# Seven block products in another order on three bank pairs, with the weight differences and loads spread over the chunks before them

## What is computed

```
def conv_glu_ffn(h_norm, w_in, conv_w, conv_b, w_out):
    gate, up = jnp.split(h_norm @ w_in, 2, axis=-1)
    ...
    return (jax.nn.silu(conv) * up) @ w_out      # 512 x 2816 times 2816 x 1024

h = h + conv_glu_ffn(rms_norm(h, norm_ffn[l]), ...)
```

## Time and profile before

| | us |
|---|---|
| median of three runs | 1417.26 |
| lowest, highest | 1415.71, 1418.31 |
| the profiled execution | 1415.03 |
| its span | 1413.3 |
| PE busy in it | 1388.4 (98%) |
| DVE, ACT, POOL busy | 879.0, 648.7, 666.3 |

### The profile page before, as it was taken

The page is one execution under the profiler, slowest core; times in us unless marked ns, Lnnn a source line. Parts: engine busy times, 40 slices in busy tenths (PEclk is TensorE's granted clock), DMA queues, the critical chain, the costliest instruction groups (busy, mean ns, idle before and its releaser), DMA issues.

```text
span 1413.3 us, 17598 instructions
## 1 busy us (share of the span) xinstructions
PE 1388.4 (98%) x6797; PEld 1135.6 (80%) x6797; DVE 879.0 (62%) x1249; ACT 648.7 (46%) x1109; POOL 666.3 (47%) x365
## 2 busy tenths in 40 slices
PE   8999999999999999999999999999999999999998
PEld 6888778887788888888888887788777878887886
DVE  4584674665776206663265656836658895888687
ACT  6747583665332212322346555735753333334333
POOL 5645663542444344444346367535344434443542
PEclk9999999999999999999999999999999999999999
DMA  6332012331233233333333210223223602530521
GB/s 175 98 99 64 27 46 75 113 111 50 86 104 105 97 92 104 96 90 98 96 90 103 86 61 16 76 71 109 90 66 91 209 24 60 181 117 1 157 67 59
DMA packets 176305, 125.67 MB, mean 89 GB/s; under 512 B 14657, under 2 KB 152672, under 8 KB 176224
## 3 DMA queue, kind: packets, MB, share of 16 engines
q1 hardware_dynamic: 175664, 124.55, 29.4%
q10 hardware_dynamic: 560, 0.01, 0.0%
HBM read 122.44 MB, written 2.10 MB: 88 GB/s over the span
## 4 chain that ended last, share of the span: by engine, by line
PE 88%; DVE 8%; ACT 1%; issue 1%; DMA 1%; SPq 0%; DVEq 0%; ACTq 0%
PE bank L751 25%; PE bank L755 25%; PE bank L753 25%; PE bank L925 2%; DVE h L1912 1%; PE bank L1054 1%; PE bank L1055 1%; PE bank L1134 1%; PE bank L913 1%; PE bank L1094 1%; DVE w_lo L1919 1%; DMA raw<-in_w_ffn_in 1%; DVE Q L2108 1%; PE bank L1209 1%; DVE h_tok L1886 1%
## 5 line engine op out<-in xcount | busy, mean ns | idle before, releaser
L674 POOL TENSOR_TENSOR w_lo<-raw,w_hi 128x1024 fp32r<-128x1024 f32 (+2 forms) x206 | 495.0, 2408 | 596.0 <-ACT w_hi L1334 594.2
L751 PE MATMUL bank<-x_hi,w_hi 128*128 128x512 f32 x944 | 371.5, 394 | 3.8 <-issue 2.5
L755 PE MATMUL bank<-x_hi,w_lo 128*128 128x512 f32 x944 | 367.6, 389 | 0.0
L753 PE MATMUL bank<-x_lo,w_hi 128*128 128x512 f32 x944 | 367.5, 389 | 0.0
L1334 ACT ACTIVATE w_hi<-raw 128x1024 fp32r<-128x1024 f32 (+2 forms) x205 | 212.9, 1040 | 245.4 <-PE bank L755 236.9
L751 PEld LDWEIGHTS bank<-x_hi,w_hi 128*128 128x128 f32 x944 | 177.3, 188 | 47.2 <-issue 7.8
L753 PEld LDWEIGHTS bank<-x_lo,w_hi 128*128 128x128 f32 x944 | 177.3, 188 | 37.6 <-issue 1.4
L755 PEld LDWEIGHTS bank<-x_hi,w_lo 128*128 128x128 f32 x944 | 177.2, 188 | 36.9
L2226 DVE SCALAR_TENSOR_TENSOR conv<-gate_in,gains_all,conv 128x512 f32<-128x512 f32 x44 | 113.4, 2577 | 1.6
L1685 ACT ACTIVATE conv_silu<-conv 128x512 f32<-128x512 f32 x44 | 27.8, 632 | 176.5 <-DVE conv L2227 176.5
L1867 DVE TENSOR_TENSOR h<-h,bank 128x512 f32<-128x512 f32 x48 | 31.8, 681 | 105.3 <-PE bank L755 105.2
(11 more groups left out here) (341 smaller groups left out, 2484.8 us busy)
## 6 DMA issues: line engine op xcount, KB each, us to landing
raw<-in_w_ffn_in SPq DMA_DIRECT2D x88, 512.0 KB, 3.9
raw<-in_w_in SPq DMA_DIRECT2D x27, 512.0 KB, 3.7
raw<-in_w_ffn_out SPq DMA_DIRECT2D x20, 512.0 KB, 3.6
raw<-in_w_mix_out SPq DMA_DIRECT2D x16, 512.0 KB, 3.8
raw<-in_w_ca_kv SPq DMA_DIRECT2D x32, 256.0 KB, 3.2
raw<-in_w_ca_q SPq DMA_DIRECT2D x8, 512.0 KB, 3.4
raw<-in_w_ca_out SPq DMA_DIRECT2D x8, 512.0 KB, 3.9
raw<-in_w_in SPq DMA_DIRECT2D x12, 256.0 KB, 2.9
```

The lines of the kernel that those rows point to most:

```text
L674: pool.tensor_tensor(w_lo[gi % SPLIT][:, c0:n], whole[:, c0:n], w_hi[gi % SPLIT][:, c0:n].bitcast(f32), ALU.subtract).then_inc(S["lo_split ...
L751: pe.matmul(o, ah, bh, start=first, stop=False, skip_group_check=shared_bank)
L753: pe.matmul(o, ah, bl, start=False, stop=False, skip_group_check=shared_bank)
L755: mm = pe.matmul(o, al, bh, start=False, stop=last, skip_group_check=shared_bank)
```

## The change

The seven products are made in another order, b11, b21, t1, t2, b22, t3, t4. The first three are made slab by slab, so that s0 of all three comes before s1 of any. Three pairs of banks are used instead of two and a half: the products of a12 and a22 have a pair of their own (banks 0, 1 or 2, 3, changing with the group, and the chunks' banks change with it), which makes one more addition to `h_tok` per row block in every group (16 instead of 14). DVE makes t1 in two pieces, after the fourth and third chunk from the end, instead of at once after the last but one; `w_lo` of t1's s0 is made inside the last chunk, ahead of `act`; t4 comes ahead of t3. SP loads b11 to b21 earlier: over chunks 3 to 6 of the first group, and chunks 1 to 3 of the others.

```
-    PRODUCTS = (("a11", "b11"), ("s1", "t1"), ("s2", "t2"), ("a12", "b21"), ("s3", "t3"), ("s4", "b22"), ("a22", "t4"))
+    PRODUCTS = (("a11", "b11"), ("a12", "b21"), ("s1", "t1"), ("s2", "t2"), ("s4", "b22"), ("s3", "t3"), ("a22", "t4"))
+    FIRST = 3
...
+    def product_slabs(g):
+        some = pair_slabs(g)
+        return [(q, s, nk) for s, nk in some for q in range(FIRST)] + [(q, s, nk) for q in range(FIRST, len(PRODUCTS)) for s, nk in some]
...
-        X_BANKS, Z_BANKS, W_BANKS = (4, 5), (6, 7), (2, 3)
+        X_BANKS, Z_BANKS, W_BANKS = (4, 5), (6, 7), ((0, 1), (2, 3))
...
+        OUT_OF = (("x", True), ("w", True), ("z", True), ("x", False), ("z", False), ("x", False), ("w", True))
+        C11, C12, C21, C22 = (0, 0), (0, 1), (2, 0), (2, 1)
+        SUMS = ((0, C11), (1, C11), (2, C22), (3, C12), (4, C12), (5, C22), (5, C21), (6, C21))
...
                     if g == 0:
-                        sp.wait_ge(S["hk_evac"], 2 * NT)
+                        sp.wait_ge(S["r_bc_done"], past(LAST, "r_bc_done") + 2)
+                        if B_HOME[name] is b_v:
+                            sp.wait_ge(S["hk_evac"], 2 * NT)
...
-                                    at = ("gate", "up")[j % 2], g, LG[g] - 2 + j // 2
-                                    if g:
-                                        at = "gate", g, LG[g] - 4 + j
+                                    at = ("gate", g, 3 + j) if g == 0 else (("up", "gate")[j % 2], g, 1 + (j + 1) // 2)
...
                         if c == LG[g] - 1:
-                            split_through(slab_of(layer, ("out", g, 1, 0)))
+                            split_through(slab_of(layer, ("out", g, 2, 0)))
...
-                        each(t_sum, "t2")
-                        for s, nk in some[1:]:
-                            t_low(g, 1, s, nk)
...
+                        for x in some:
+                            t_sum(g, "t2", *x)
+                        t_low(g, 2, *last)
                         add_product(g, 0)
...
+                        t_low(g, 3, *some[0])
                         add_product(g, 1)
-                        each(t_sum, "t4")
+                        for x in some:
+                            t_sum(g, "t4", *x)
+                        t_low(g, 3, *last)
                         add_product(g, 2)
-                        each(t_low, 4)
+                        for x in some:
+                            t_sum(g, "t3", *x)
                         add_product(g, 3)
...
                             link(dve.tensor_tensor(up_s[n % 2][:, :], pb[b + 1][:, :], r_bc[:, :], ALU.mult))
+                            before_act()
                             dve.wait_ge(S["silu_done"], past(layer, "silu_done") + 2 * n + 2)
...
-                                if c == LG[g] - 2:
-                                    for s, nk in pair_slabs(g):
-                                        t_sum(g, "t1", s, nk)
+                                if c in (LG[g] - 4, LG[g] - 3):
+                                    t_sum(g, "t1", *some[c - LG[g] + 4])
```

More of the change, by code:

```diff
@@ L215, in build_trunk @@
             ffn_in_slabs(g, c, LG_FIRST[g] + c)
-        for q, (_, b) in enumerate(PRODUCTS):
-            for s, nk in pair_slabs(g):
-                slab(("out", g, q, s), nk, HALF, (b, g, s))
+        for q, s, nk in product_slabs(g):
+            slab(("out", g, q, s), nk, HALF, (PRODUCTS[q][1], g, s))
     layer_slabs = [plain_slabs] * LAST + [slabs]
@@ L568, in _ @@
                             small_rows()
-                for q, t0, half in ((3, 0, 0), (4, 2, 1), (5, 0, 1), (6, 2, 0)):
+                for a in (1, 4, 5, 7):
+                    t0, half = SUMS[a][1]
                     for i in range(2):
-                        sp.wait_ge(S["c_added"], c_adds(len(LG) - 1, q, i))
+                        sp.wait_ge(S["c_added"], c_adds(len(LG) - 1, a, i))
                         c = slice(half * HALF, (half + 1) * HALF)
@@ L1260, in _ @@
                                 n = LG_FIRST[g] + c
-                                b = 2 * (n % 2)
+                                b = glu_bank(g, c)
                                 evacs = [(S[e], past(layer, e) + n + 1) for e in ("gate_ready", "act_ready")]
@@ L1271, in _ @@
                                     turn_back((n - 1, n))
-                            for q in range(len(PRODUCTS)):
-                                out_product(g, q)
+                            for q, s, nk in product_slabs(g):
+                                out_product(g, q, s, nk)
                         continue
@@ L1876, in add_product @@
                     def add_product(g, q):
[L1878 to L1884, removed]
-                            c = slice(half * HALF, (half + 1) * HALF)
-                            dve.tensor_tensor(h_tok[:, t0 + i, c], h_tok[:, t0 + i, c], pb[banks[i]][:, :], ALU.add).then_inc(S["c_added"], 1)
+                        for a, (r, target) in enumerate(SUMS):
+                            if r != q:
+                                continue
+                            t0, half = target
+                            before = [j for j in range(a) if SUMS[j][1] == target]
+                            for i in range(2):
+                                if before:
+                                    dve.wait_ge(S["c_added"], c_adds(g, before[-1], i))
+                                elif g:
+                                    dve.wait_ge(S["c_added"], c_adds(g - 1, max(j for j in range(len(SUMS)) if SUMS[j][1] == target), i))
+                                dve.wait_ge(S["out_mm"], 2 * (len(PRODUCTS) * g + q) + i + 1)
+                                c = slice(half * HALF, (half + 1) * HALF)
+                                dve.tensor_tensor(h_tok[:, t0 + i, c], h_tok[:, t0 + i, c], pb[banks_of(g, q)[i]][:, :], ALU.add
+                                                  ).then_inc(S["c_added"], 1)
                     def b_ready(g, name):
@@ L1908, in t_sum @@
                             b_ready(g, "b21")
-                            dve.wait_ge(S["t_lo"], t_los[slab_of(layer, ("out", g, 1, s))])
+                            dve.wait_ge(S["t_lo"], t_los[slab_of(layer, ("out", g, 2, s))])
                             dve.wait_ge(S["t_done"], t_count(g, "t2", s))
```

56 lines of the change are left out of this document (28 added, 28 removed).

## The result

The changed kernel takes 1426.08 us (median of 4 runs, 1423.43 to 1428.05), the kernel before 1416.49 in the same comparison: ratio 1.0067, 95% interval 1.0045 to 1.0090, 9.6 us slower by the medians. The forecast, 1422 with a range up to 1426, has the sign and about half the size; the measured time stands at the very end of the range. The profiled execution took 1425.97 us, its span is 1424.2, 10.9 longer than before.

What follows compares the result with a forecast made beforehand. PE, busy 98%, bounds the kernel, so only its 12.4 us of out-stage waits could be won. Terms -0.4 + 1.85 + 1.65 + 1.7 = +4.8 us on 1415.03 give 1419.8; the median, 2.2 above, 1422; range 1417 to 1426.

Steps and rivals of the forecast that it cites:

- the exclusion: DVE's instructions with two SBUF inputs and POOL's take turns, each for a whole instruction; t2's subtractions take 3.4 us, not 1.1.
- The rival "faster": In the out stages the exclusion doesn't bite in the new places: 9.1 us less, 1408; chance 0.15.
- b11's s1: Out stage opening, groups of eight: due T+8.16 from stage start T, ready T+9.8; a wait of 1.7 us.
- b21's s1: Groups of eight: POOL's second slab lets a t2 subtraction go first, ready T+13.2, due T+12.8; 0.6 us.
- the slow pair: After a PE wait the first matmul or two run slower; counted as 0.2 us for each wait.
- the group of six: Third out stage: waits sum to 5.7 us, the longest 3.7 at t2's s1; 34.3 us, +1.65.
- t2's s1 in the groups of eight: t4's subtractions stand ahead of its `w_lo`: ready T+22.4, due T+21.6, counted as 1.0 us.
- the refinement: A DVE instruction queued directly behind another keeps the turn if it waits for at most one semaphore; with several it loses it.
- the "worse" rival: Groups of eight: POOL beats t4's second subtraction, so t2's s1 waits 2.4 us longer in each: 1427; chance 0.05.
- b22's s1: Groups of eight: POOL waits for t4, t2, then t3; ready T+29.0, due T+28.0; 1.4 us.
- the first group: -0.4 forecast: First out stage: 43.0 us like the second group, -0.4 against before, if the clock stays up.
- the clock in the third group: Third out stage: one stretch at the lower clock, where PE stands still for 3.7 us; +1.7 us.

Runs made afterwards that it cites:

- small b22 kernel: Changed kernel, but POOL writes only 16 of the 1024 or 512 `w_lo` columns for b22's slabs: 1414.81 us.
- the one that splits twice: Changed kernel, but in the groups of eight ACT writes `w_hi` of b22's s0 twice, so POOL starts that slab 1.0 us later: 1422.20 us.
- t1 late: Changed kernel, but t1's two subtractions go back together behind the last chunk but one: 1422.68 us.
- both: Changed kernel with t1's `w_lo` back just ahead of the last `p_lo` and t2's s1 `w_lo` ahead of t4's subtractions: 1415.06 us.
- t3 first: Changed kernel with DVE's t4 subtractions put last, behind t3's; t1's `w_lo` stays ahead of `act`: 1415.47 us.
- all: Changed kernel with t4's subtractions last on DVE and t1's `w_lo` back just ahead of the last `p_lo`: 1411.53 us.

## Why the forecast was right, and where it was too small

*Right: the exclusion, and what it does in the new places.* The small b22 kernel and the one that splits twice change only what POOL does or when, and DVE's `w_lo` of t2's s1 goes from 3.38 to 1.2 us. t2's subtractions took the forecast 3.4 us each. The rival "faster" rested on their staying at 1.2; it is out.

*Right: b11's s1 by the chain over `act`, `p_hi` and ACT's split.* Forecast 1.7, measured 1.64 in the second group; gone there when t1's `w_lo` goes back. *Right:* b21's s1, 0.31 for 0.4 without the slow pair; the group of six, where the longest wait is 3.55 for 3.7. Of the stages that the forecast named as its signs, 43, 43 and 34 to 36 us, only the second comes near (46.58, 43.79, 37.25).

*Mis-sized, t2's s1 in the groups of eight: 0.8 forecast, 2.86 measured in both.* The step that failed is the refinement that "an instruction of DVE that is queued directly behind another and waits for at most one semaphore keeps the turn". I had it from a `w_lo` for which POOL came 0.19 us before it was due to start. In the group of six of the kernel before, timelines of DVE and POOL show a second case:

```profile
1387.68 1.82 DVE L1912 TENSOR_TENSOR b_y<-b_z,b_y 128x1024 f32<-128x1024 f32 x2
1389.42 0.68 DVE L1919 TENSOR_TENSOR w_lo<-b_x,w_hi 128x512 fp32r<-128x512 f32 x1
...
1388.38 6.21 POOL L674 TENSOR_TENSOR w_lo<-h,w_hi 128x1024 fp32r<-128x1024 f32 x2 [13.89 <-ACT w_hi L1334]
```

There the second subtraction was due at 1387.68 + 1.14 = 1388.82, 0.44 us after POOL's arrival, and kept the turn. The small b22 kernel has a third, in its first group:

```profile
1165.10 2.35 DVE L1933 TENSOR_TENSOR b_y<-b_z,b_y 128x1024 f32<-128x1024 f32 x2
...
1165.59 1.95 POOL L689 TENSOR_TENSOR w_lo<-b_z,w_hi 128x16 fp32r<-128x16 f32 x1 [1.52 <-ACT w_hi L1348]
```

The second subtraction of t3 was due at 1165.10 + 1.14 = 1166.24, 0.65 us after POOL's arrival, and kept the turn too: POOL's 16 columns were done only at 1167.54. In the changed kernel POOL came 1295.67 - 1294.76 = 0.91 us ahead, and the `w_lo`, with one semaphore to wait for, lost it. So the turn is kept only against a late arrival; the limit lies somewhere between 0.65 and 0.91 us, if it is the same for these instructions, and no run here places it closer. The other half of the refinement holds: t2's first subtraction, which waits for more than one semaphore, lost its turn to a POOL that came 1282.08 - 1281.86 = 0.22 us ahead. I named a race at this place as the "worse" rival (1427), by another instruction (t4's second subtraction) and with 5% only. It came close to that rival's price, 2.1 us a group where I had 2.4, and my sum had not counted on it. The Trainium skill, "SBUF — State Buffer", section "Who interferes with whom", which lets whoever issues first have one whole instruction, gave 43.9 us for the groups of eight; the trace has 43.79 in the second, so here the page's plain rule did better than mine, while it misses the old order's kept turns. The wait at t2's s1 cost 2.0 us more than forecast, but made PE late enough for b22's s1, forecast at 1.4: the second group is 43.79 for 43.0. That it comes so near is partly luck, two errors that cancel.

*Mis-sized, the first group: -0.4 forecast, +3.20 measured.* I took it to be like the second, and the clock to stay up. It is 46.58 - 43.79 = 2.79 us longer. Some 1.7 of that is half of a 3.4 us stretch at the lower clock behind the wait at t2's s1. The rest, 1.2, is b11's s1, 2.82 for 1.64. Timelines of DVE and POOL of the changed kernel in the last chunk of that group:

```profile
1136.34 2.45 DVE L2242 TENSOR_SCALAR conv<-gate_in,gains_all 128x512 f32<-128x512 f32 x1
1138.83 2.76 DVE L2244 SCALAR_TENSOR_TENSOR conv<-gate_in,gains_all,conv 128x512 f32<-128x512 f32 x1
...
1136.12 2.40 POOL L687 TENSOR_TENSOR w_lo<-b_x,w_hi 128x1024 fp32r<-128x1024 f32 x1 [4.80 <-ACT w_hi L1346]
1138.47 2.58 POOL L687 TENSOR_TENSOR w_lo<-h,w_hi 128x1024 fp32r<-128x1024 f32 x1
```

Both slabs that POOL has under this chunk (b11's s0 as before, b21's s0 new there) hold up a step of the convolution, and `act` starts at T+4.4 instead of T+3.2. In the second group POOL's first slab came 1.2 us earlier by the stage's start; there the TENSOR_SCALAR took 1.26 us, and only the second step was held up as long. The trace of the kernel before could have warned me: its `act` in the first group, too, starts 2.2 us later by the stage's start (T+3.7) than in the second (T+1.5).

```profile
1144.10 0.69 DVE L2232 TENSOR_TENSOR act<-conv_silu,up_s 128x512 f32<-128x512 f32 x1 [0.17 <-ACT conv_silu L1685]
```

Why DVE enters the last chunks of the first group later, in both kernels, was not tried. With t1 late it was still so (3.50 us), so t1's spreading is not the reason.

*Mis-sized, the clock in the third group: 1.7 forecast, 2.8 measured.* Behind the 3.55 us wait 14 matmuls stand 0.43 us apart instead of 0.23, 1404.3 to 1410.3, nearly twice the stretch that I had counted. 34.3 + 2.8 = 37.1 for 37.25.

Sum of the terms as measured: 0.49 + 3.20 + 2.64 + 4.57 = 10.9 for the forecast 4.8. Of the 6.1 us between them, 3.6 lie in the first group, 0.8 in the second, 1.2 in the third and 0.5 ahead of the stages. The range held because it left room for two more falls of the clock, and about as much did come, one in the first group and a longer one in the third, though not behind the waits of 1.7 us that I had named; for the turns lost at t2's s1 it had left none.

Two readings in the forecast are not exact. Only one of POOL's instructions, b11's s1, moves from under the last chunk into the out stage; b21's s1 comes there from further back. And in the group of six T+20.4 less T+16.9 is 3.5 us, not 3.7.

*What it says of the change.* The new order of products was not what cost the time. With the same order, banks and loads, and only a few of DVE's instructions placed elsewhere, it is 14.5 us faster than as it was made, and 4.7 us faster than the old one. The cost was in two places: a `w_lo` ahead of `act`, on which the first late slab hung, and t4, needed last, ahead of t2's s1, needed next. Mended singly they gave 4.0 and 10.6 us, both at once 14.5.

## What to carry to other kernels

Where two engines exclude one another for whole instructions, do not ask how much work each has, but which instruction loses the turn, and who waits for it: put the instruction that PE needs next ahead of the other engine's arrival, and let those that are needed late lose. A race of that kind moves with anything that delays one of the two engines alone, so a timetable that is right to some tenths of a us is worth more than a sum of busy times. Laid out before the runs, it gave the second group's stage as 41.0, 41.4 and 39.8 us in the three kernels for which the length is on record (both, t3 first, all), and 40.85, 41.30 and 39.70 were measured; for the third group it gave 33.0, 33.1 and 32.0, and 33.05, 33.13 and 32.00 were measured. It was 1.4 us short in the first group of two of them (42.37 and 42.75 for 41.0 and 41.4), where DVE comes late, and it missed where PE's clock fell and moved POOL.

## What the runs showed of the hardware that was not expected

A longer wait did not always bring the lower clock. Of PE's waits in the out stages of the twelve profiles (before, changed, ten experiments), none under 1.8 us was followed by a stretch at the lower clock; of 13 from 1.8 to 3.1 us five were (the shortest 1.99, while one of 3.09 was not); all five of 3.5 us and more were. The same wait in the same kernel, 2.86 us at t2's s1, was followed by one in the first group and not in the second. Such a stretch costs about 1.7 us where it is 3.4 us long, and more where it is longer. They seem to be a part of why the runs of one kernel differ by some us: over the 54 runs of the kernel before that stand beside the experiments, time and mean granted clock go together (correlation -0.7). Where in those runs the clock fell, in these stages or elsewhere, is not shown.

A fall of the clock can pay for itself: with t1 late, in the second group, it cost PE some 1.7 us and, by making POOL late as well, took away a wait of 2.86 (42.88 us for 43.79).
